# A hybrid decoder step on one core: the first norm taken on rows, and the FFN norm's root multiplied in behind the weights

## The chip, the cores and the metric

One core of a Trainium2 chip runs one launch of the kernel. The metric is the device time of a launch in microseconds. A few engines are named throughout: TensorE (PE; PEld is its weight load), VectorE (DVE), ScalarE (ACT), GpSimd (POOL) and SyncE (SP), whose queue issues most DMAs.

## The reference

The reference is one layer of a decoder for 512 prompt tokens and 8 sample tokens (T = 520), in float32, with D = 1024 and D_FF = 2816. What the change touches is this:

```python
def rmsnorm(x, g, eps=1e-6):
    return x * rsqrt(mean(x * x, axis=-1) + eps) * g

xn = rmsnorm(x, norm_mix);  z = xn @ W_in          # 4 branches, gates: o_A .. o_D
x  = x + (sum_i sigmoid(gate_i) * (o_i @ W_branch_i)) @ W_out
x  = x + CrossAttn(rmsnorm(x, norm_cross), memory)  # ends with @ w_co
g, u = split(rmsnorm(x, norm_ffn) @ w_ffn_in)
x  = x + (silu(causal_dwconv3(g)) * u) @ w_ffn_out
y  = rmsnorm(x, norm_final)
```

The last rows of g before the convolution are an output too (the state of the FFN convolution). For a sample token the convolution's history comes from an input state.

## The kernel before, in words

Activations lie transposed: a tile has 128 channels on the partitions and all 520 tokens on the free axis, and `xT` holds the residual as 8 such tiles (index k). Every matrix product is made in "pieces": 128 columns of a weight matrix against all tokens, with the sum over up to 8 k. Weights (`raw`) and activations are each split in a rounded high part and a low part (the difference), and each k takes three products: high by high, high by low, low by high (L919 to L921). A piece with 8 k is thus 2 halves of 260 tokens x 24 products. ScalarE rounds the weights (`split`, L1171 to L1177), GpSimd or, for some kinds, VectorE subtracts (L776, L1662), two pieces ahead. The accumulators `pb` are two tiles of two halves, so tile m can start when tile m - 2 has been read out. The other PSUM tensor `sd` (its quarters are `s0` to `s3`) serves everything else.

The order of all work is written out in one list, `timeline()` (L216 to L340), that each engine's program walks and from which it takes its own part: `piece`, `evac` (read a tile out), `evac2` (its second step), `side` (one of the small steps of the list `SIDE`, L165), `nsq`, `nroot` and `napply` (a norm's squares, root and application), `tap`, `k` and `v` (one tap of a long convolution, one page of a cache). After each half piece one side step is taken. Each engine is strictly in this order. Pieces 0 to 3 are "fq", 4 to 11 "cv" and "cg", 12 to 23 "gx"; 132 to 139 are "co" (w_co, 4 k each), 140 to 183 alternate two "fg" (gate) and two "fu" (up) tiles of the FFN, and 184 on are "fo".

The prologue: SP loads the constants' first 256 columns, four row tiles of x (512 KB each, `xrow`), x_sample, the other constants, and the parameter rows (L676 to L701), then the weights. TensorE transposes x and the parameters through `sd` (L831 to L846) and VectorE copies them to `xT` and `cols` (L1950 to L1961). Then norm 0 runs: ScalarE squares each k (L1249), TensorE sums over the partitions with a matrix of ones (L863 to L868), ScalarE takes Ln and Exp (L1256, L1257), and per k VectorE multiplies x, gain and root, ScalarE rounds to `xh`, VectorE subtracts to `xl` (L1642 to L1650). Piece 0 waits per k for `xl`. The residual is stored to a scratch in HBM (L1511), as its place holds other things in between.

Side steps "sm" 0 to 3 compute the decay and gate scalars from 16 columns of w_in: 48 products, transposes, a chain on VectorE and ScalarE. They start at piece 2. "fqr" sends the sample's queries to HBM behind piece 4; GpSimd reads them back, and with them the cache pages' products (L791) and sums on VectorE (L1686) can start.

Norms 2 to 4 (`ADDED`) square on ScalarE, add on VectorE (`n_add`, L1979) and let TensorE sum only once. For norm 3, the squares of tile k come behind the read-out of "co" tile k; the last square, the root and the nine apply steps stand before the first "fg" piece (L299 to L301). An "fg" tile is read out by ScalarE three times (tail, times the last tap, plain copy for the conv; L1215 to L1220), then VectorE's conv (L1638), tanh on ScalarE (L1188), a product (L1597), and the "fu" tile's product with it (L1640), rounded and subtracted to `hh` and `hl`.

## Time and profile before

| | |
|---|---|
| median of 3 runs | 1775.3 us (1775.08 to 1779.56) |
| the profiled execution's own time | 1775.84 us |
| its span, first to last instruction | 1773.0 us |
| mean granted TensorE clock | 0.91 of full |
| TensorE busy | 1512.1 us, 85% |
| VectorE busy | 918.6 us, 52% |
| ScalarE busy | 581.3 us, 33% |
| GpSimd busy | 557.2 us, 31% |

The stages follow each other, so a share over the whole span says little; what binds is read stage by stage. Times in the trace are microseconds from the span's start. TensorE's matmul rows show a duration with the pipeline's fill; what a product costs in a stream is the distance of two starts, or a stretch over its count.

### The profile page before, as it was taken

How to read it: one execution, taken by the hardware profiler on the slowest of the kernel's cores; microseconds unless marked ns; L12 is line 12 of the kernel's file. 1: busy time of each engine (PE TensorE's matmuls, PEld its weight loads, DVE VectorE, ACT ScalarE, POOL GpSimd, SP SyncE). 2: the span in 40 equal slices, each digit the busy share in tenths (PEclk: the TensorE clock that was granted, in tenths of full speed). 3: DMA queues.
4: the chain of work that ended last, by engine and by line, in shares of the span. 5: the costliest groups of instructions: out<-in, count | busy, mean ns of one | idle time of the engine just before them, and what ended most of it. 6: DMA issues, size and time to landing. Idle time of an engine off the chain costs nothing. (4 is left out here: it accounts for less than half of the span.)

```text
span 1773.0 us, 28178 instructions
## 1 busy us (share of the span) xinstructions
PE 1512.1 (85%) x11047; PEld 1396.2 (79%) x11047; DVE 918.6 (52%) x1286; ACT 581.3 (33%) x918; POOL 557.2 (31%) x310
## 2 busy tenths in 40 slices
PE   4886878688897988799888889888676999999995
PEld 3886877688897988776656659888566999999995
DVE  5159896889968675433233332264335555552112
ACT  3322560212133223433221232444324334433222
POOL 2255545343342333011111014310412444343440
PEclk9898996899998999899888879999877999999998
DMA  7144523433342444267544426433322333332331
GB/s 220 48 111 121 144 74 89 126 105 107 105 146 84 143 113 136 56 193 223 145 129 125 137 74 198 126 95 107 114 66 66 90 96 96 89 91 79 91 99 49
DMA packets 254643, 199.83 MB, mean 113 GB/s; under 512 B 15780, under 2 KB 212957, under 8 KB 254104
## 3 DMA queue, kind: packets, MB, share of 16 engines
q1 hardware_dynamic: 234149, 169.47, 33.1%
q10 hardware_dynamic: 19371, 23.86, 4.1%
q0 software_dynamic: 992, 4.72, 0.8%
q8 instruction: 87, 1.43, 0.3%
q14 instruction: 44, 0.36, 0.1%
HBM read 187.89 MB, written 10.81 MB: 112 GB/s over the span
## 5 line engine op out<-in xcount | busy, mean ns | idle before, releaser
L822 PE MATMUL pb<-xh,wh 128*128 128x260 f32 x2176 | 650.7, 299 | 51.7 <-DVE xl L1555 22.6
L822 PE MATMUL pb<-xl,wh 128*128 128x260 f32 x2176 | 634.2, 291 | 0.0
L822 PE MATMUL pb<-xh,rawl 128*128 128x260 f32 x2176 | 632.5, 291 | 0.0
L776 POOL TENSOR_TENSOR rawl<-raw,wh 128x1024 fp32r<-128x1024 f32 (+2 forms) x152 | 339.4, 2233 | 909.5 <-ACT wh L1169 908.7
L822 PEld LDWEIGHTS pb<-xh,wh 128*128 128x128 f32 x2176 | 431.4, 198 | 66.5 <-issue 44.3
L822 PEld LDWEIGHTS pb<-xl,wh 128*128 128x128 f32 x2176 | 431.8, 198 | 0.7
L822 PEld LDWEIGHTS pb<-xh,rawl 128*128 128x128 f32 x2176 | 430.4, 198 | 0.0
L1169 ACT ACTIVATE wh<-raw 128x1024 fp32r<-128x1024 f32 (+2 forms) x208 | 201.6, 969 | 545.0 <-PE pb L822 493.4
L822 PE MATMUL sd<-ar 128*128 128x128 f32 (+7 forms) x1488 | 262.7, 389 | 95.6 <-DVE ar L1555 62.3
L822 PEld LDWEIGHTS sd<-ar 128*128 128x128 f32 (+4 forms) x1488 | 178.9, 193 | 141.0 <-issue 75.8
L791 POOL TENSOR_TENSOR ar<-ar 128x512 f32<-128x512 f32 x128 | 189.0, 1476 | 248.9 <-DMA ar<-in_cache_fox_k 226.1
L1575 DVE SCALAR_TENSOR_TENSOR ar<-ar,cols 128x512 f32<-128x512 f32 x88 | 93.8, 1066 | 72.5 <-ACT ar L1169 71.8
L822 PE MATMUL pb<-oh,wh 128*128 128x260 f32 (+1 forms) x384 | 119.0, 310 | 9.2 <-ACT ar L1169 7.2
L1679 DVE SCALAR_TENSOR_TENSOR ar<-xT,cols,ar 128x512 f32<-128x512 f32 x120 | 125.7, 1085 | 1.2
L822 PE MATMUL pb<-ol,wh 128*128 128x260 f32 (+1 forms) x384 | 113.2, 295 | 0.0
L822 PE MATMUL pb<-oh,rawl 128*128 128x260 f32 (+1 forms) x384 | 113.0, 294 | 0.0
L1662 DVE TENSOR_TENSOR rawl<-raw,wh 128x1024 fp32r<-128x1024 f32 (+1 forms) x56 | 68.3, 1219 | 79.2 <-ACT wh L1169 79.1
L822 PE MATMUL pb<-hh,wh 128*128 128x260 f32 x352 | 101.5, 288 | 2.6 <-DVE hl L1555 2.6
L822 PE MATMUL pb<-hh,rawl 128*128 128x260 f32 x352 | 100.7, 286 | 0.0
L822 PE MATMUL pb<-hl,wh 128*128 128x260 f32 x352 | 100.6, 286 | 0.0
L826 PE MATMUL sd<-cst,ar 128*128 128x128 f32 (+7 forms) x359 | 65.0, 305 | 41.7 <-ACT ar L1476 18.5
L1686 DVE TENSOR_REDUCE ar<-ar 128x8 f32<-128x512 f32 x128 | 84.8, 678 | 26.9 <-POOL ar L791 26.0
(174 smaller groups left out, 1685.8 us busy)
## 6 DMA issues: line engine op xcount, KB each, us to landing
raw<-in_w_in SPq DMA_DIRECT2D x80, 512.0 KB, 4.2
ar<-in_cache_fox_k SPq DMA_DIRECT2D x128, 256.0 KB, 2.8
ar<-in_cache_fox_v SPq DMA_DIRECT2D x128, 256.0 KB, 3.0
raw<-in_w_ffn_in SPq DMA_DIRECT2D x44, 512.0 KB, 3.9
raw<-in_w_branch SPq DMA_DIRECT2D x32, 256.0 KB, 3.1
raw<-in_w_ffn_out SPq DMA_DIRECT2D x16, 512.0 KB, 3.9
ar<-in_cache_mem_k ACTq DMA_DIRECT2D x1, 4096.0 KB, 19.1
raw<-in_w_out SPq DMA_DIRECT2D x8, 512.0 KB, 3.9
```

The lines of the kernel that those rows point to most:

```text
L776: pool.tensor_tensor(rawl[:, p % RING, 0:kt, :], raw[:, p % RING, 0:kt, :], wh[:, p % (AHEAD + 1), 0:kt, :].bitcast(F32), SUB).then_inc(lo ...
L791: own(pool.tensor_tensor(kring[:, i % 4, :], kring[:, i % 4, :], qb[:, :], MUL), prod_done)
L822: return pe.matmul(o, l, r, start=start, stop=stop, skip_group_check=True)
L826: return pe.transpose(o, i, ident[0:n, 0:n])
L1169: own(act.activation(o, i, f, **kw), st)
L1575: (st if j == width - 2 else dve_c).by(dve.scalar_tensor_tensor(out=y[:, 0:SEQ], in0=x[:, 4 - width + j:4 - width + j + SEQ], scalar=wcol( ...
L1662: dve.tensor_tensor(rawl[:, p % RING, 0:kt, :], raw[:, p % RING, 0:kt, :], wh[:, p % (AHEAD + 1), 0:kt, :].bitcast(F32), SUB).then_inc(lo. ...
L1679: dve_c.by(dve.scalar_tensor_tensor(out=oC[:, c, 0:SEQ], in0=g[:, j - 1:j - 1 + SEQ], scalar=w[:, j - 1:j], in1=oC[:, c, 0:SEQ], op0=MUL, ...
L1686: page_free.by(dve.tensor_reduce(sc[:, i, :], kring[:, i % 4, :].rearrange("p (h d) -> p h d", h=FH), AX, ADD))
```

## The change

Two edits.

**First norm.** SP loads the vectors and two weight tiles before the other constants. ScalarE squares each row tile of x with a sum along the row, takes the root of the 5 columns of sums, and ScalarE and VectorE scale the rows into a new tensor `xnr`. TensorE transposes the scaled rows into `pb`; ScalarE reads them with the gain into `xh`, VectorE computes gain times the same minus `xh` into `xl`. TensorE's transposes of the parameters follow, and only then piece 0. The raw residual is transposed in new side steps "xr" 0 to 5 behind pieces 2 to 4, in the place of "sm", which goes behind "fqr". The store to the scratch is in "xr" 5.

**FFN norm.** Without its root, the norm's apply is a gain per channel. It is done tile by tile behind the read-out of "co" (`gain`), so the FFN's products run on x times gain. The squares' sum and the root are taken behind the first half of the first "fg" piece. Every "fg" tile is multiplied with the root (`lrsx`) as VectorE reads it from PSUM, and the product silu(g) once more with the root, for the sake of u. The tail and the scaled copy move from ScalarE to VectorE.

The diff, cut to its core:

```diff
-BY_ACT = {"fq", "fk", "fv", "cv", "cg", "gx", "ac", "gateA", "gateB", "gateC", "gateD", "gz", "kv", "cq", "fg"}
+BY_ACT = {"fq", "fk", "fv", "cv", "cg", "gx", "ac", "gateA", "gateB", "gateC", "gateD", "gz", "kv", "cq"}
...
-SIDE = ([("AFTER", "fq", 0)] + [("sm", n) for n in range(4)]
+SIDE = ([("AFTER", "fq", 0)] + [("xr", n) for n in range(6)]
         + [("AFTER", "fq")] + [("fqr", n) for n in range(2)] + [("KSTART",)]
+        + [("sm", n) for n in range(4)]
...
-    norm(0)
...
         if p == first_piece("fg"):
+            out.append(("gain", KD - 1))
             out.append(("nsq", 3, KD - 1))
-            norm(3, False)
...
             if kind == "co" and h == 1 and p > first_piece("co"):
+                out.append(("gain", p - first_piece("co") - 1))
                 out.append(("nsq", 3, p - first_piece("co") - 1))
+            if p == first_piece("fg") and h == 0:
+                out.append(("nsum", 3))
+                out.append(("nroot", 3))
...
+            own(pool.memset(zsam[:, :], 1.0), pool_made)
```

TensorE's prologue and the new side step:

```diff
+            pe.wait_ge(vec_in, 16 * 11)
+            pro_pe.by(tr(s3[:, 0:P], pv[:, B_VEC, :]))
+            pe.wait_ge(row_act.sem, 3)
+            for k in range(KD):
+                last = tr(s2[:, k * NB:(k + 1) * NB], xnr[0:NB, QT, k * P:(k + 1) * P])
+            pro_pe.by(last)
+            pe.wait_ge(row_dve.sem, 2)
+            for k in range(KD):
+                if k >= 4:
+                    pe.wait_ge(n_lo.sem, k - 3)
+                for t in range(QT):
+                    last = tr(pb[:, k % 4 // 2, k % 2, t * P:(t + 1) * P], xnr[:, t, k * P:(k + 1) * P])
                 pro_pe.by(last)
+            pe.wait_ge(par_in, 16 * 7)
+            for j in range(5):
+                if j == 2:
+                    pe.wait_ge(n_lo.sem, 1)
+                if j == 3:
+                    pe.wait_ge(pro_dve.sem, 1)
+                if j == 4:
+                    pe.wait_ge(n_lo.sem, KD)
+                for b in range(max(1, 4 * j), 4 * j + 4):
+                    last = tr((sd[:, j, :] if j < 4 else pb[:, 1, 1, :])[:, (b % 4) * P:(b % 4 + 1) * P], pv[:, b, :])
+                pro_pe.by(last)
...
+                if kind == "xr":
+                    for j in range(2):
+                        for t in range(QT):
+                            tr(sd[:, j, t * P:(t + 1) * P], xrow[:, t, (2 * n + j) * P:(2 * n + j + 1) * P])
+                        last = tr(s2[:, j * NB:(j + 1) * NB], xsrow[0:NB, (2 * n + j) * P:(2 * n + j + 1) * P])
```

ScalarE:

```diff
+            def gain(k):
+
+                if k == 0:
+                    act.wait_ge(kprod.sem, NB)
+                act.wait_ge(ev_all.sem, count(dve_tile, mt_of("co", k)))
+                n_hi.by(act.activation(xh[:, k, :], xT[:, k, :], ACT.Copy, scale=col(V_FFN + k)))
...
+            for t in range(QT):
+                act.wait_ge(x_in[t], 16)
+                act_c.by(act.activation(xnr[:, t, :], xrow[:, t, :], ACT.Square, accum_out=ssq[:, t:t + 1]))
+            act.wait_ge(x_in[QT], 16)
+            fn(xnr[0:NB, QT, :], xsrow[0:NB, :], ACT.Square, accum_out=ssq[0:NB, QT:QT + 1])
+            fn(rsq, ssq, ACT.Ln, scale=1.0 / D, bias=eps6[:, 0:1])
+            fn(rsq, rsq, ACT.Exp, row_rt, scale=-0.5)
+            row_act.by(act.activation(xnr[:, 0, :], xrow[:, 0, :], ACT.Copy, scale=rsq[:, 0:1]))
+            row_act.by(act.activation(xnr[0:NB, QT, :], xsrow[0:NB, :], ACT.Copy, scale=rsq[0:NB, QT:QT + 1]))
+            row_act.by(act.activation(xnr[:, 2, :], xrow[:, 2, :], ACT.Copy, scale=rsq[:, 2:3]))
+            split(0)
+            act.wait_ge(xs_gain.sem, 1)
+            fn(xh[:, :, SEQ:T], xsg, ACT.Copy, xs_gain)
+            for k in range(KD):
+                if k == 2:
+                    split(1)
+                act.wait_ge(pro_pe.sem, 3 + k)
+                n_hi.by(act.activation(xh[:, k, 0:SEQ], pb[:, k % 4 // 2, k % 2, :], ACT.Copy, scale=col(V_MIX + k)))
```

VectorE, the read-out of an "fg" tile, the new side step, the prologue and the gain:

```diff
                     elif kind == "fg":
-                        stt(pairA[:, s, :], pairB[:, s, :], 1.0, pairA[:, s, :], ADD, MUL, ev_all)
+                        stt(pairA[:, s, :], pairB[:, s, :], 1.0, pairA[:, s, :], ADD, MUL)
+                        tt(pairA[:, s, :], pairA[:, s, :], lrsx[:, :], MUL, ev_all)
...
                 elif kind == "fg":
+                    tt(both(cb[:, s, 3:3 + T]), x, both(lrsx[:, :]), MUL, mt_dve)
+                    cp(tail_ff[:, idx, :], cb[:, s, 3 + T - 10:3 + T])
+                    ts(pairA[:, s, :], cb[:, s, 3:3 + T], cols[:, B_FW, 2 * KF + idx:2 * KF + idx + 1])
                     conv(cb[:, s, :], pairA[:, s, :], FCW, lambda j: cols[:, B_FW, KF * j + idx:KF * j + idx + 1], fh[:, :, :, idx], ev_y)
...
+                if kind == "xr":
+                    for j in range(2):
+                        dve_c.by(dve.tensor_copy(xT[:, 2 * n - 2 + j, 0:SEQ], sd[:, j, :]))
...
+            for t in (1, 3):
+                row_dve.by(dve.tensor_scalar(xnr[:, t, :], xrow[:, t, :], rsq[:, t:t + 1], None, MUL))
...
+            for k in range(KD):
+                dve.wait_ge(n_hi.sem, k + 1)
+                n_lo.by(dve.scalar_tensor_tensor(out=xl[:, k, 0:SEQ], in0=pb[:, k % 4 // 2, k % 2, :], scalar=col(V_MIX + k),
+                                                 in1=xh[:, k, 0:SEQ].bitcast(F32), op0=MUL, op1=SUB))
...
+                elif e[0] == "gain":
+                    k = e[1]
+                    dve.wait_ge(n_hi.sem, 3 * KD + k + 1)
+                    stt(xl[:, k, :], xT[:, k, :], col(V_FFN + k), xh[:, k, :].bitcast(F32), MUL, SUB, n_lo)
```

## Rows read from the trace of the kernel before

**Rows 1.** Busy time by stage: stretch, its length, each engine's us (instructions), clock, DMA.

```profile
0.00:38.80 38.80, 17.23 (x92) 14.52 (x92) 17.91 (x31) 13.98 (x18) 8.89 (x14) 0.98 0.75 217
110.00:200.00 90.00, 69.72 (x514) 68.27 (x513) 86.74 (x89) 25.68 (x39) 54.60 (x30) 0.89 0.47 132
1318.00:1338.00 20.00, 20.00 (x168) 19.83 (x166) 11.40 (x19) 9.53 (x14) 10.45 (x7) 1.00 0.48 141
1380.00:1480.00 100.00, 100.00 (x840) 100.00 (x840) 51.86 (x51) 38.99 (x58) 41.86 (x18) 1.00 0.32 92
```

**Rows 2.** Timeline of the prologue: start, us, engine, line, operation, count, idle before.

```profile
10.79 7.08 PE L826 MATMUL sd<-cst,ar 8*128 8x8 f32 x40 [10.79 <-DMA ar<-in_x_sample]
32.37 1.28 ACT L1169 ACT_TABLE_LOAD   x1 [1.28 <-PE pb L822]
34.38 1.28 ACT L1169 ACT_TABLE_LOAD   x1
38.86 0.56 PE L822 MATMUL pb<-xh,wh 128*128 128x260 f32 x1 [6.57 <-DVE xl L1555]
48.75 0.57 PE L822 MATMUL pb<-xh,wh 128*128 128x260 f32 x1
49.99 0.42 PE L822 MATMUL pb<-xh,rawl 128*128 128x260 f32 x1
50.20 0.42 PE L822 MATMUL pb<-xh,wh 128*128 128x260 f32 x1
```

**Rows 3.** Line 826, PE, two stretches: duration ns min/median/max, first and last start.

```profile
L826 PE MATMUL sd<-cst,ar x20: 420/421/474, 11.7 to 15.8; 128*128 128x128 f32 x20
...
L826 PE MATMUL sd<-cst,ar x20: 272/273/300, 19.3 to 21.4; 128*128 128x128 f32 x20
```

**Rows 4.** Timeline between 78 and 109 us, TensorE, VectorE, ScalarE.

```profile
78.76 1.51 PE L822 MATMUL sd<-ar,cst 8*128 8x128 f32 x5 [3.46 <-DVE ar L1555]
...
106.03 0.69 DVE L1686 TENSOR_REDUCE ar<-ar 128x8 f32<-128x512 f32 x1 [21.88 <-POOL ar L791]
...
109.03 1.06 ACT L1169 ACTIVATE wh<-raw 128x1024 fp32r<-128x1024 f32 x1 [4.03 <-PE pb L822]
```

**Rows 5.** Timeline under w_co and up to the first FFN pieces.

```profile
1318.00 0.70 DVE L1561 SCALAR_TENSOR_TENSOR xT<-pb,xT 128x520 f32<-128x520 f32 x1 [3.38 <-PE pb L822]
...
1327.36 0.15 DVE L1564 COPY cols<-cols 128x1 f32<-128x1 f32 x1
1327.69 0.64 ACT L1249 ACTIVATE ar<-xT 128x520 f32<-128x520 f32 x1 [0.42 <-DVE cols L1564]
...
1333.53 2.42 POOL L776 TENSOR_TENSOR rawl<-raw,wh 128x1024 fp32r<-128x1024 f32 x1 [2.02 <-ACT wh L1169]
1334.23 2.27 DVE L1555 TENSOR_TENSOR ar<-ar 128x520 f32<-128x520 f32 x1 [0.96 <-ACT ar L1249]
...
1337.76 0.28 PE L822 MATMUL pb<-oh,rawl 128*128 128x260 f32 x1
1341.18 0.70 DVE L1555 TENSOR_TENSOR ar<-ar 128x520 f32<-128x520 f32 x1 [0.91 <-ACT ar L1249]
1341.94 2.10 PE L822 MATMUL sd<-ar,cst 128*128 128x260 f32 x4 [3.90 <-DVE ar L1555]
...
1366.13 1.06 ACT L1169 ACTIVATE wh<-raw 128x1024 fp32r<-128x1024 f32 x1 [5.41 <-PE pb L822]
```

**Rows 6.** DMA, first 40 us: GB/s in slices; one issue, its size.

```profile
GB/s 0 27 189 305 306 403 382 400 391 309 398 229 191 174 132 199 96 93 277 307 299 301 291 290 299 345 380 320 260 21 0 0 0 0 0 0 0 532 266 532
...
cst<-in_cst SPq DMA_DIRECT2D x1, 836.0 KB
```

**Rows 7.** VectorE: line 1671 (520 columns scaled), and two instructions of the timeline.

```profile
L1671 DVE TENSOR_SCALAR ar<-xT,cols x4: 549/549/1453, 115.6 to 341.5; 128x520 f32<-128x520 f32 x4
...
1350.50 0.76 DVE L1561 SCALAR_TENSOR_TENSOR ar<-xT,cols,ar 128x520 f32<-128x520 f32 x1
...
1414.40 1.63 DVE L1575 SCALAR_TENSOR_TENSOR ar<-ar,cols 128x512 f32<-128x512 f32 x1 [3.81 <-ACT ar L1169]
```

More of the change, by code:

```diff
@@ L198, in sums_before @@
 def sums_before(i):
-    return sum(1 if n in ADDED else KD for n in range(i))
+    return sum(1 if n in ADDED else KD for n in range(1, i))
 def adds_before(i):
@@ L583, in build @@
         pv = v(QKV, N_BLK, P)
[L584 removed]
+        xnr, xrow, xsrow = v(0, 5, D), v(G + 1600, QT, D), v(8800, D)
+        ssq, rsq, xsg = zsam[:, 0:5], zsam[:, 8:13], v(SQ, KD, NB)
         wsm = v(G, KD, 16)
@@ L722, in v_group @@
                     page("cache_fox_v", i, v_slot(i), v_in[i % 8])
-            for p in range(RING - 1):
+            for p in range(2, RING - 1):
                 weights(p)
@@ L936, in side @@
                     return
-                if sums[0] > 1 and kind != "ef":
+                if sums[0] and kind != "ef":
                     pe.wait_ge(n_rt.sem, sums[0])
@@ L1281, in side @@
                 kind, n = s[0], s[1]
-                works = act_works(s) or s in (("gs", 8), ("ml", 0)) or (kind == "x" and n > 0)
+                works = act_works(s) or s in (("gs", 8), ("ml", 0), ("xr", 5)) or (kind == "x" and n > 0)
                 if not works:
@@ L1290, in side @@
                 va, av = upto(to_act, K), upto(to_dve, K)
-                if kind == "sm" and n == 1:
+                if kind == "xr":
+                    store(xscr, xT[:, :, :].rearrange("p a b -> p (a b)"), xs_out)
+                elif kind == "sm" and n == 1:
                     fins = act.activation(both(zrow[0:16, :]), sd[0:16, 2:4, 0:TH], ACT.Copy)
```

153 lines of the change are left out of this document (68 added, 85 removed).

## The prediction

> **What bounds the kernel now.** I read the execution by stages first. TensorE is all but full in the FFN (100 us of work in 100 us), VectorE fills the stretch from 110 to 200 us, and TensorE does 17.2 us of work in the first 38.8 us [rows 1]. So an end-to-end gain is a start that comes earlier or a hole in TensorE that closes; anything added to VectorE is free only where it has room. The two edits lie at two such holes.
>
> The first hole is the prologue. The reader is to see in the timeline that TensorE begins at 10.79 us, when x_sample, the last of the rows of x, has landed, and that the first product with weights starts at 38.86 us. Its first half piece (24 products) takes until 48.75 us, because each k waits for one gain, one rounding and one subtraction, and only from there do the products follow closely [rows 2]. They do so at 0.21 us each at first (50.20 less 49.99) [rows 2], against 0.119 us each in the FFN (100 us over 840) [rows 1]: half the granted clock. The transposes show the same two levels, 420 and 272 ns [rows 3]. TensorE finishes piece 7 at about 109.0 us, where ScalarE's rounding of weights is released [rows 4].
>
> The second hole is the norm before the FFN. The last product of w_co starts at 1337.76 us, the sum over partitions at 1341.94 us, and the first FFN piece is done only at 1366.1 us, where the rounding that waits for it starts [rows 5]. A piece of 48 products needs 5.7 us.
>
> **The prologue, part by part.** *Removed:* eight squares, 32 float32 products of 260 columns, a root on 520 columns with two table loads of 1.28 us, and the k-by-k apply [rows 2]. *Added on rows:* five squares of 1024 columns with a sum, a root of 5 columns, five scalings shared by ScalarE and VectorE, 40 transposes into PSUM, and eight times a gain by ScalarE and a subtraction by VectorE that both read PSUM. *Moved:* 40 transposes of the raw rows with their copies go to side steps behind pieces 2 to 4; the four gate-weight steps go behind fqr.
>
> When does the dense work start? The loads of x are 2.1 MB behind 128 KB; the first nine slices of 1 us in the traffic row sum to some 2.7 MB, of which a part was the 836 KB of constants that now go last [rows 6]. I take x as landed at 9.0 us (bounds 8.5 and 10.8, the time of before). Then on ScalarE: two squares 2.1 us, two table loads and two short functions 3.0, three scalings 3.2 (each 1.06, the duration of 128x1024 in [rows 5]): 17.3 us. VectorE's two scalings (1.1 each, twice the 549 ns of 520 columns [rows 7]) end earlier. Eight small transposes and the sample's gain take 1.2 us: 18.5. The eight k are then paced by the slowest of three: TensorE 0.85 us at the lower clock for four transposes (7.08 us for 40 with their copies [rows 2]), ScalarE 0.65 plus one rounding of weights (1.06) between, VectorE 0.76 [rows 7]. That is 8 x 0.8 + 1.06 + 1.4 for the ends of the pipe = 8.9: the eighth low part at 27.4. Four parameter transposes that wait for it take 0.5 to 0.9: **first piece at 28.3 us**, dense at once, as all eight k are there. TensorE has then worked for about 9 us almost without a hole; in the kernel of before the same kind of start gave the fast transposes by 19.3 us [rows 3], so I take the higher clock, and add 1 us for what may be left of the lower.
>
> From there to the end of piece 7: 384 products x 0.119 = 45.7 us; the 40 raw transposes at the higher clock 4.4 us (0.11 each for 19 of [rows 3], twice that at the lower clock); and the gate-weight steps as they cost now. From 48.75 to 109.0 are 60.3 us, in which 24 products at the lower and 336 at the higher clock take 5.1 + 40.0; the other 15.2 are those steps with 48 products, a 3.46 us hole [rows 4] in which TensorE waits for the chain on VectorE and ScalarE, and the lower clock behind it. I take the hole unchanged, as the chain is the same and has one half piece of cover in both orders. Sum: 28.3 + 1 + 45.7 + 4.4 + 15.2 = 94.6 us against 109.0, **14.4 us earlier**. Bounds: 10 us (x at 10.8, chain slower by 2, low clock for 24 more products) and 18 us (no clock loss, shorter loads).
>
> Does this reach the end? VectorE's full stretch begins with the first page sum at 106.03 us [rows 4], fed by the query row that fqr writes, which is still behind piece 4, so it moves with TensorE. The 3.4 us of gate arithmetic that VectorE now does inside pieces 6 and 7 falls where it waited for that query, so I cost it at nothing; without this cover it costs 3.4 us. In the other direction TensorE reaches fqr still earlier than piece 8, which could hide the query's round trip: up to 3 us more, kept for the range. SP's queue now passes two weight loads ahead of the constants: needed at 26 us, loaded in the first 20 or so. The store of x for the scratch is needed only by the first memset, two pieces later. The added GpSimd memset of 16 columns is nothing.
>
> **The FFN norm, part by part.** *Removed:* nine apply steps between w_co and the FFN, and the wait for the root. *Added under w_co:* per tile one gain on ScalarE (0.64) and one subtraction on VectorE (0.76 [rows 7]). VectorE's chain per tile becomes 0.70 accumulate, 0.15 copy, 0.1, 0.64 gain, 0.1, 0.76 subtraction, 0.70 add and 0.1 between: 3.3 us [rows 5, 7]. TensorE gives a tile every 2.87 us (24 x 0.119). So VectorE falls behind, and it is late next.
>
> There is a second cost. At 1334.23 us a VectorE add of two SBUF operands took 2.27 us where the same takes 0.70, and it ended just behind a GpSimd subtraction that ran from 1333.53 for 2.42 us; the evacuations, which read PSUM, keep their 0.70 [rows 5]. So each of the two added SBUF instructions can be held up. The Trainium skill has this as a rule against the change (GPSIMD Engine Reference, section 2, Architecture, and SBUF — State Buffer, section "SBUF: two separate sides"): the two engines share a pair of SBUF ports under an exclusive lock, and a VectorE instruction with two SBUF inputs is fully blocked while GpSimd holds it. By that rule the trace agrees.
>
> I walked the eight tiles through with the GpSimd subtractions set 0.75 us behind each release of ScalarE: evacuations start at 1318.0 [rows 5], 1321.4, 1324.6, 1327.9, 1331.2, 1334.4, 1338.4 and 1342.1 (3.44 us apart; two of them held by the long weight subtractions). The last low part is there at 1344.6, TensorE has waited 3 us for it, the sum over partitions costs 1.0 (half of 2.10, which was at the lower clock [rows 5]) plus 0.7 wait, and 27 products 3.2: first piece done at 1349.5, with 0.8 for clock 1350.1 against 1366.1: **16 us earlier**. Bounds: 20.5 (no lag: w_co's end plus 5.7 and the sum), and 8 (every added instruction held, 4.2 us a tile, and the lower clock after it).
>
> *Added per gate tile of the FFN on VectorE:* a product from PSUM with the root (0.70), a tail copy, a scaling (0.55), a product of two SBUF tiles (0.70). Four pieces take 22.9 us; VectorE's two gate and two up tiles then need some 16 us with the ScalarE waits between, and its conv step is held to 1.63 us by GpSimd already now [rows 7]. A gate tile's PSUM is wanted back 5.7 us after its evacuation can start; the second of a pair is delayed by the first to about 3 us. So this costs nothing, by the cover of that 2.6 us; if it is gone, TensorE stops once per pair, 11 times. ScalarE gets three instructions fewer per tile. The root (two loads and 1.3 us, 4.0 in all) ends under piece 1.
>
> **Sum.** 14.4 + 16 = 30.4 us off the profiled execution of 1775.8 us: 1745.4. That execution is 0.5 us above the median of 1775.3, so the median goes to **1745 us** (1.7% faster).
>
> A second rule of the skill, on table loads (ScalarE: Activation LUTs, "What ACT_TABLE_LOAD costs"), puts a drain of about 1.38 us onto each 1.28 us load. With it the two loads of the row root would cost 2.8 us more and the sum be 27.6 us. The trace has the second load begin 2.01 us after the first, with the first's own 1.28 and a whole activation in between [rows 2]: no run here shows room for that drain, and the traced 1.28 stands. Either sum lies inside the forecast's own range below.
>
> **The rivals.**
> (a) *VectorE bound under w_co:* every added instruction is held, as the one of 2.27 us. For it: GpSimd works 10.45 of 20 us there [rows 1]. Against: in my walk VectorE often starts first. FFN gain 8: total 23 us, 1752.
> (b) *The early start is partly lost:* x lands no earlier, the clock is low into piece 0, and gate arithmetic queues behind the page sums on VectorE, which then holds TensorE's step: prologue gain 8, total 24, 1751. It covers also that a moved step simply meets the same wait later.
> (c) *The change doesn't do what it says in one half:* the norm of rows is as long as the old one, since rows need two passes over ScalarE. Total 16 to 18, 1758. Against: the sum over partitions and the slow apply (9.9 us for a half piece) do go.
> (d) *Slower:* the lock in each FFN cycle. Per four pieces GpSimd works 9.6 us (41.86 per 100 [rows 1]); if VectorE did nothing meanwhile and lost 0.5 us behind each hold, it would need 9.6 + 16 + 2.5 = 28 us for 22.9: 5.2 us x 11 = 57 us lost, 1802 in all. It decides for slower from 2.8 us per cycle (30.4 / 11). Against: half of VectorE's instructions read PSUM, and one that starts first should finish first. (That a held VectorE instruction waits for the whole of GpSimd's is what the skill's SBUF page says of the lock; taken at every instruction, it gives this case.)
> (e) A mild form of (d), 1 us per cycle: gain 20, 1755.
>
> **How the numbers follow.** Forecast (1738 to 1750) 0.6; (a) 0.12; (b) 0.1; (e) 0.06; (c) 0.05; (d) 0.03; still better than 1738 through the hidden query 0.04. Range 1737 to 1756: from both upper bounds nearly together with the query's 3 us (18 + 18 + 3) to (a) and (b) with a part of (e). Faster by over 0.3% (5.3 us, about what a measurement of this kernel can tell from no change) 0.94: all but (d) and the tails of (c) and (e), which give within 0.02 and, with (d), slower 0.04.
>
> **What would show it.** First product with weights near 28 us and close spacing at once; piece 7 done near 95 us; first FFN piece done some 16 us less late against w_co's start; evacuations of w_co 3.3 to 3.7 us apart; the FFN at 840 products per 100 us. Wrong if TensorE's share in the FFN falls below 98%, or if the stretch from piece 7 to w_co grows.

## The result and the profile after

The changed kernel takes **1734.25 us** (median of 4 runs, 1732.22 to 1735.71) beside 1775.19 for the kernel before (4 runs, 1773.79 to 1779.56): a ratio of 0.9765, 95% interval 0.9744 to 0.9785. The forecast was 1745 with a range from 1737 to 1756, so the change gained more than the range allowed. Repeated later (experiment h1), it took 1739.24 us (6 runs, 1730.57 to 1744.83), ratio 0.9806 [0.978, 0.9832]. All ten runs together have their median at 1735.4, the 15 runs of the kernel before that stood beside them at 1773.5: **38 us** gained, of 30.4 forecast. The profiled execution took 1732.22 us, its span is 1729.2.

Busy time by stage of the kernel after, answering to [rows 1]; the columns are the same, the second and third stretch lie 14 and 27 us earlier, as the work does:

```profile
0.00:38.80 38.80, 20.58 (x148) 19.75 (x149) 15.60 (x31) 23.17 (x34) 13.84 (x17) 1.00 0.78 210
96.00:186.00 90.00, 71.62 (x529) 70.31 (x527) 86.57 (x87) 27.51 (x40) 53.48 (x28) 0.89 0.45 128
1291.00:1311.00 20.00, 20.00 (x165) 19.89 (x164) 12.94 (x23) 12.59 (x19) 9.09 (x6) 0.98 0.45 131
1380.00:1480.00 100.00, 100.00 (x841) 100.00 (x840) 73.23 (x89) 30.59 (x36) 42.73 (x17) 1.00 0.31 91
```

The FFN is as full as before (841 products in 100 us), though VectorE now works 73.2 us of 100 in place of 51.9.

Timeline of the prologue of the kernel after, ScalarE and TensorE (start, us, engine, line, operation, count, idle before), with the end of piece 7 as its last row; it answers to [rows 2, 4]:

```profile
5.36 1.28 ACT L1529 ACT_TABLE_LOAD   x1 [5.36 <-DMA ar<-in_x_prompt]
6.65 1.06 ACT L1529 ACTIVATE ar<-ar 128x1024 f32<-128x1024 f32 x1
...
10.80 0.19 ACT L1529 ACTIVATION_READ_ACCUMULATOR ar<-ar 128x1 f32 x1
...
12.04 1.28 ACT L1195 ACT_TABLE_LOAD   x1
13.34 0.30 ACT L1195 ACTIVATE ar<-ar 128x5 f32<-128x5 f32 x1
13.66 1.28 ACT L1195 ACT_TABLE_LOAD   x1
...
28.32 0.37 PE L836 MATMUL pb<-xh,wh 128*128 128x260 f32 x1
28.52 0.28 PE L836 MATMUL pb<-xl,wh 128*128 128x260 f32 x1
28.64 0.28 PE L836 MATMUL pb<-xh,rawl 128*128 128x260 f32 x1
...
95.18 1.06 ACT L1195 ACTIVATE wh<-raw 128x1024 fp32r<-128x1024 f32 x1 [1.27 <-PE pb L836]
```

The first product with weights starts at 28.32 us, from the second on the products follow at 0.12 us, and piece 7 is done at 95.18 in place of 109.03: 13.9 us earlier.

Under w_co, VectorE, GpSimd, TensorE and ScalarE of the kernel after; it answers to [rows 5]:

```profile
1307.98 2.41 POOL L790 TENSOR_TENSOR rawl<-raw,wh 128x1024 fp32r<-128x1024 f32 x1 [2.29 <-ACT wh L1195]
1309.73 1.21 DVE L1605 SCALAR_TENSOR_TENSOR xl<-xT,cols,xh 128x520 fp32r<-128x520 f32 x1 [0.93 <-ACT xh L1284]
...
1315.25 0.70 DVE L1605 SCALAR_TENSOR_TENSOR xT<-pb,xT 128x520 f32<-128x520 f32 x1
1317.07 0.76 DVE L1605 SCALAR_TENSOR_TENSOR xl<-xT,cols,xh 128x520 fp32r<-128x520 f32 x1 [0.92 <-ACT xh L1284]
1317.88 0.39 PE L836 MATMUL pb<-xh,wh 128*128 128x260 f32 x1 [2.45 <-DVE xl L1605]
1318.62 1.69 PE L836 MATMUL sd<-ar,cst 128*128 128x260 f32 x4
...
1324.36 1.06 ACT L1195 ACTIVATE wh<-raw 128x1024 fp32r<-128x1024 f32 x1
```

The eight evacuations start between 1291.39 and 1315.25 us, 3.41 apart; TensorE waits 2.45 us for the last low part, and the rounding behind the first FFN piece starts at 1324.36.

To find the surplus I lined the two traces up by the starts of ScalarE's 208 roundings of weights (counted from 0 like the pieces; the nth is that of piece n's weights and stands two pieces ahead of it) and took the difference. It is 13.9 us at the 10th, 15.7 at the 96th, 20.3 at the 100th, 23.5 at the 131st, 25.6 at the 140th, 41.8 at the 143rd and 44.6 at the 207th. The two steps that were forecast are there (13.9, and 16.2 from the 140th to the 143rd). Nearly 12 us stand between the 10th and the 140th, where the diff seems to touch nothing. I call these 12 us the surplus.

### The profile page after: what moved, and what is told of

The parts are those of the page before. It is cut to its first block and busy times, and to the rows that moved or that the text cites. A ratio compares the mean times of both kernels' runs of the same rounds, so it can differ in the third digit from the quotient of the medians.

```text
span 1729.2 us, 28170 instructions
## 1 busy us (share of the span) xinstructions
PE 1486.3 (86%) x11055; PEld 1379.2 (80%) x11055; DVE 961.7 (56%) x1366; ACT 556.1 (32%) x858; POOL 563.1 (33%) x311
## 5 line engine op out<-in xcount | busy, mean ns | idle before, releaser
L836 PE MATMUL pb<-xh,wh 128*128 128x260 f32 x2176 | 642.0, 295 | 34.1 <-ACT ar L1195 16.6
L790 POOL TENSOR_TENSOR rawl<-raw,wh 128x1024 fp32r<-128x1024 f32 (+2 forms) x152 | 343.9, 2263 | 859.1 <-ACT wh L1195 858.5
L836 PEld LDWEIGHTS pb<-xh,wh 128*128 128x128 f32 x2176 | 425.1, 195 | 42.0 <-issue 28.7
L836 PEld LDWEIGHTS pb<-xl,wh 128*128 128x128 f32 x2176 | 425.3, 195 | 0.5
L836 PEld LDWEIGHTS pb<-xh,rawl 128*128 128x128 f32 x2176 | 424.7, 195 | 0.0
L836 PE MATMUL sd<-ar 128*128 128x128 f32 (+7 forms) x1488 | 258.8, 390 | 95.9 <-DVE ar L1599 63.3
L840 PE MATMUL sd<-cst,ar 128*128 128x128 f32 (+6 forms) x363 | 63.7, 291 | 48.9 <-ACT ar L1505 20.7
## 6 DMA issues: line engine op xcount, KB each, us to landing
ar<-in_cache_mem_k ACTq DMA_DIRECT2D x1, 4096.0 KB, 19.7
```

Source lines behind the costliest of these rows:

```text
L790: pool.tensor_tensor(rawl[:, p % RING, 0:kt, :], raw[:, p % RING, 0:kt, :], wh[:, p % (AHEAD + 1), 0:kt, :].bitcast(F32), SUB).then_inc(lo ...
L836: return pe.matmul(o, l, r, start=start, stop=stop, skip_group_check=True)
L840: return pe.transpose(o, i, ident[0:n, 0:n])
```

## The experiments

Time is the median, the ratio is to the kernel before with its 95% interval; a gain in us behind a ratio is worked out from the ratio, unless it says medians. The kernel before was run again beside each group of experiments, with medians from 1771.0 to 1776.1 us, so two times of different groups compare only within a few us. The letters of the theories are those of each run's expectation. For the first four runs, theory A tied the surplus to the early start, and theory B to something that does not depend on it (in e1 and e2, to the FFN edit).

**e1: the rows edit alone** (the FFN norm, its apply and the readers of the "fg" tiles as before).

```diff
-            out.append(("gain", KD - 1))
             out.append(("nsq", 3, KD - 1))
+            norm(3, False)
```

> Only the first norm on rows and the moved side steps; the FFN norm and the read-out of the gate tiles are as before. The two edits' own gains in the traces are 13.9 us (piece 7 done at 95.2 instead of 109.0 us) and 15.2 us (between w_co and the first FFN pieces), 29 of the 41 us. Theory A (TensorE's clock falls at other places once everything starts at another time, and that gives the other 12 us): up to the FFN this kernel starts each stage as the changed one does, so it is 14 us plus about 9 us faster than before: ratio 0.987. Theory B (the other 12 us belong to the FFN edit): 14 us, ratio 0.992.

Measured: 1752.72 us, ratio 0.9876 [0.9848, 0.9905], 22 us off (19.7 by medians): more than theory B's 14.

**e2: the FFN edit alone** (the prologue and the side steps as before).

```diff
-            norm(3, False)
+            out.append(("gain", KD - 1))
...
             if kind == "co" and h == 1 and p > first_piece("co"):
+                out.append(("gain", p - first_piece("co") - 1))
```

> Only the FFN edit on the kernel before: gains under w_co, root behind the first half piece, gate tiles multiplied with it. Theory A: the stages ahead of the FFN are untouched and start when they did, so the gain is the edit's own 15 us, or up to 18 with the clock drop at the FFN's end avoided: ratio 0.990 to 0.9915. Theory B: 15 + 12 = 27 us, ratio 0.985. If both edits' gains simply add up, this one and e1 give 41 us together.

Measured: 1758.87 us, ratio 0.9901 [0.987, 0.9932], 17.5 us off (13.6 by medians; its six runs span 1748.3 to 1762.5). In its trace the difference to the kernel before is -1.0 us at the 140th rounding and 14.9 at the 143rd: nothing in the middle. The surplus comes with the rows edit.

**e3: the changed kernel, started late.** Thirteen more squares of 1.06 us before the row root.

```diff
+            for _ in range(13):
+                fn(xnr[:, 0, :], xrow[:, 0, :], ACT.Square)
             fn(rsq, ssq, ACT.Ln, scale=1.0 / D, bias=eps6[:, 0:1])
```

> The changed kernel with 13 squares of a row tile (1.04 us each plus waits, about 14 us) more on ScalarE ahead of the row root, thrown away. Every stage from piece 8 to w_co then starts about when it started before the change. Theory A (the start time decides where the clock falls): the delay costs 14 us and gives the extra back: 22 to 26 us slower than the changed kernel, ratio to before about 0.990. Theory B (the extra belongs to the new order of steps, not to the start time): it costs just 14 us, ratio 0.984 to 0.985.

Measured: 1753.50 us, ratio 0.9884 [0.9858, 0.991], 19.3 us over the changed kernel's first 1734.25, but 14.3 over its repeat. By the times this decides nothing. Its trace does: piece 7 ends at 110.24 us, 1.2 later than before, and at the 100th rounding this kernel is still 7.7 us ahead. Theory A falls for most of the surplus.

**e4: the kernel before, once more.**

> The kernel before once more, for a second trace of it. If the places where TensorE's clock falls repeat from run to run, each stage's time and granted clock is within 1 us and 0.02 of the first trace (971.7 to 1056.2 at 0.78; the FFN's end 1600.9 to 1629.9 at 0.88). If they are chance, they differ by several us from stage to stage, and the total by up to the 6 us that its four runs span.

Measured: 1773.65 us, ratio 1.0002 [0.9983, 1.002]. Its trace and the first one of the same kernel drift up to 5 us apart and are within 1 us at the end. A single rounding's difference of less than that means nothing.

What e1, e3 and the changed kernel share against e2, e4 and the kernel before is the list of side steps. The planner emits an event of the cache's value pages ("v", a group of four; "vx", a row's end) at each side step but every seventh: `background("v", step_n[0] % 7 > 0)`. The change puts six new steps ("xr") in front. So the count is six higher at each later step, other steps are the seventh, and six page events (groups 0, 5, 10, 15 and 24 and the end of one row, in pieces 77 to 95) come half a piece earlier. The prediction did not follow this count.

**f1: the kernel before, with the page events of the changed one.**

```diff
-                background("v", step_n[0] % 7 > 0)
+                background("v", (step_n[0] + 6) % 7 > 0)
```

> The kernel before, with one number of the planner changed: the value pages of the cache are skipped at every seventh side step, and the count is moved on by six, as the six new side steps of the change do. So the six page events that the change moves by half a piece (four pages and the end of one row's query among them, in pieces 77 to 95) stand where they stand in the changed kernel; nothing else is changed. Theory P (the extra gain of the middle comes from this move): 9 us off, 1772.5 to about 1763.5, ratio 0.993 to 0.997, and the rounding of weights 100 comes about 8 us earlier than in the kernel before. Theory S (it comes from the earlier start, or from TensorE's clock falling elsewhere): within 2 us of the kernel before, ratio 0.999 to 1.001.

Measured: 1767.85 us, ratio 0.998 [0.9964, 0.9996], 3.5 us off (0.7 to 6.4): between theory P's 0.993 to 0.997 and theory S's 0.999 to 1.001, so the time alone settles little. The stretch where the traces part shows more. From the 98th rounding to the 100th TensorE does the last page steps, and behind piece 96 all that are left in one burst. Waits of TensorE's weight loads there, first the kernel before (engine, line, releaser: us in total, times, longest):

```profile
PEld sd L822 <- ACT ar L1359: 8.0, 3, 3.8
PEld sd L822 <- DMA ar<-in_cache_fox_v: 2.6, 2, 1.4
PEld sd L826 <- ACT ar L1359: 2.2, 1, 2.2
```

and f1:

```profile
PEld sd L822 <- ACT ar L1359: 7.7, 3, 3.8
PEld sd L826 <- ACT ar L1359: 2.4, 1, 2.4
```

TensorE's matmuls wait another 0.7 us for the same DMA before, and not at all in f1. It is the last group, 31. At event n SP loads group n + 1, once TensorE has used group n - 1 (L754 to L757 of the changed kernel), so group 31 is loaded when group 29 is used. Group 29's is a seventh event that moves, inside the burst, ahead of step "fox" 31 in place of behind it. TensorE's timeline before, where group 29's eight products are in the row of 12 at 1036.11:

```profile
1029.33 0.64 PE L822 MATMUL sd<-ar 128*128 128x128 f32 x2
1032.07 2.04 PE L822 MATMUL sd<-ar 64*128 64x512 f32 x2 [2.11 <-DVE ar L1555]
...
1036.11 2.89 PE L822 MATMUL sd<-ar 128*128 128x128 f32 x12
...
1046.90 1.02 PE L822 MATMUL sd<-ar 128*8 128x512 f32 x2 [0.24 <-DMA ar<-in_cache_fox_v]
```

and in f1, where they are in the row of 10 at 1027.27 (a row names the form of its first product only):

```profile
1027.27 1.36 PE L822 MATMUL sd<-ar 128*128 128x128 f32 x10
1029.76 1.09 PE L822 MATMUL sd<-ar 64*128 64x512 f32 x2 [1.13 <-DVE ar L1555]
...
1031.96 0.61 PE L822 MATMUL sd<-ar 128*128 128x128 f32 x4
```

Before, the last page of group 31 lands at 1046.85 us and TensorE takes it at 1046.90; in f1 it has landed at 1037.07. The six moves of half a piece bring nothing that shows: f1 leads the kernel before by 0.9 us at the 10th rounding, by 1.1 at the 98th and by 6.6 at the 100th.

The DMA waits are not the whole difference. The 185th of TensorE's 258 products in this stretch starts 45.1 us into it before and 42.6 in f1, and no DMA wait has come by then; group 29's products have filled a part of the wait for VectorE. So 2.5 of the 5.5 us come ahead of the DMA waits and 2.9 with them. The stretch as a whole, first before and then f1 (columns as in [rows 1]), has a lower granted clock before:

```profile
998.15:1056.23 58.08, 48.28 (x262) 30.27 (x255) 20.64 (x40) 12.01 (x23) 2.52 (x2) 0.79 0.40 122
997.07:1049.68 52.61, 43.20 (x262) 28.87 (x255) 20.63 (x40) 12.00 (x24) 2.53 (x2) 0.84 0.41 121
```

How much of either part is the wait itself and how much the clock, the runs do not separate.

**f2: the changed kernel, with the old page events** (`(step_n[0] + 1) % 7 > 0`).

> The changed kernel with the count of side steps put back by six where the value pages are skipped, so that each page event stands in the half piece where it stands in the kernel before. Theory P: the changed kernel's 1734.3 becomes about 1743 (8 to 10 us more; ratio to before 0.981 to 0.983), what the prediction had forecast for the whole change. Theory S: 1734.3 within 2 us, ratio 0.976 to 0.978.

Measured: 1738.34 us, ratio 0.9816 [0.9786, 0.9847]: 4.1 us over the changed kernel's first median, 0.9 under its repeat. The times alone leave it open. The stretch does not:

| 98th to 100th rounding | us |
|---|---|
| old page places: before, e4, e2, f2, h2 | 58.1, 59.3, 57.6, 57.8, 57.5 |
| new places: after, h1, e1, e3, f1 | 52.5, 52.7, 52.5, 52.7, 52.6 |

No kernel of one group comes near the other: **4.8 to 6.8 us**, some 5.5, with either prologue and either FFN, early or late. The edited variants below that keep the new places (f4, g1 to g3, h3, h4, i1, i2) have 52.5 to 52.7 there too. So theory P is shown for this stretch.

**f3: a page event at every side step** (`background("v", 1)`, on the changed kernel).

> The changed kernel with a value page at every side step and none skipped: the pages run up to four events further ahead, and fewer are left for the burst behind piece 96, where TensorE waits for VectorE's rounding of them. Theory P: the burst is shorter by the events that it no longer holds; some 5 us faster than the changed kernel, 1729 (ratio 0.972 to 0.976), or a loss if a page is asked for before it is loaded. Theory S gives no reason for a difference: 1734 within 2.

Measured: 1761.64 us, ratio 0.9927 [0.9898, 0.9955]: 26 us over the changed kernel's 1735.4. The 84th to the 92nd rounding now take 114 us in place of 104, and TensorE waits for the cache's DMA there too (4.7 us). Theory P had allowed for a loss if a page is asked for before it is loaded. So the place of the pages matters on both sides.

**f4: four more products behind each gate tile of the FFN**, with the changed kernel. My forecast had priced the FFN at nothing.

```diff
+                        for _ in range(4):
+                            tt(tmp, pairA[:, s, :], lrsx[:, :], MUL)
                         tt(pairA[:, s, :], pairA[:, s, :], lrsx[:, :], MUL, ev_all)
```

> The changed kernel with four more VectorE products of two operands in SBUF (128x520, 0.70 us each, into a scratch tile) behind each gate tile of the FFN, 5.6 us for every four pieces of 22.9 us. VectorE is busy 74.1 of 100 us there, 17.0 per four pieces, so it would be busy 22.6 of 22.9. Theory A (the FFN has this room and the lock on the shared ports costs nothing while it has): 0 to 10 us more in all, 1734 to 1744. Theory L (the lock already takes most of the room, so that VectorE loses more than its own time to GpSimd's 9.8 us of each cycle): at least 2.5 us per cycle over 11 cycles, 1762 or more.

Measured: 1825.32 us, ratio 1.0303 [1.0279, 1.0326]: 90 us over the changed kernel's 1735.4, 8.2 us for each of the 11 cycles of four pieces, in which VectorE got 5.6 us of work. That is theory L's side, and far beyond its 2.5 us.

**g1: VectorE pipelined under w_co.** Its subtraction and added square of tile k stand behind the evacuation of tile k + 1.

```diff
+            order, held = [], []
             for e in TIMELINE:
+                late = e[0] == "gain" and e[1] < KD - 1 or e[0] == "nsq" and e[1] == 3 and e[2] < KD - 1
+                (held if late else order).append(e)
+                if e[0] == "evac2" and MT_KIND[e[1]] == "co":
+                    k = PIECES[MT_LAST[e[1]]][4]
+                    order += [x for x in held if x[-1] < k]
+                    held = [x for x in held if x[-1] >= k]
+            for e in order:
```

> The changed kernel; under w_co VectorE alone takes the low part and the added square of tile k behind the evacuation of tile k+1, so that it never waits for ScalarE's gain of the tile it has just evacuated. Per tile that is 0.70 + 0.15 + 0.76 + 0.70 and some 0.15 between, 2.46 us, less than TensorE's 2.87. Theory A (VectorE's chain of 3.41 us per tile is what TensorE waits 2.45 + 0.80 us for at the first FFN piece): evacuations 2.87 us apart but where GpSimd holds one, and some 3 us less in all, 1731 (ratio to before 0.974 to 0.976). Rival L (the lock is what spaces them): they stay 3.3 or more apart and the time stays at 1734 within 1.

Measured: 1739.05 us, ratio 0.9835 [0.982, 0.9851]: no gain. Timeline of g1 under w_co, GpSimd, VectorE, TensorE:

```profile
1310.26 5.19 POOL L790 TENSOR_TENSOR rawl<-raw,wh 128x1024 fp32r<-128x1024 f32 x2 [2.21 <-ACT wh L1195]
1310.30 2.92 DVE L1605 SCALAR_TENSOR_TENSOR xl<-xT,cols,xh 128x520 fp32r<-128x520 f32 x1
1313.25 2.75 DVE L1599 TENSOR_TENSOR ar<-ar 128x520 f32<-128x520 f32 x1
1316.04 0.70 DVE L1605 SCALAR_TENSOR_TENSOR xT<-pb,xT 128x520 f32<-128x520 f32 x1
...
1317.00 0.36 PE L836 MATMUL pb<-xh,wh 128*128 128x260 f32 x1 [2.64 <-DVE xT L1605]
```

Neither theory was right as written. The evacuations before this are 2.5 to 3.4 us apart, so the chain did get shorter. But VectorE no longer waits for ScalarE while GpSimd works. It runs into both of GpSimd's long subtractions and loses 2.2 and 2.1 us, another 0.9 to 1.0 us behind each of three short ones, and TensorE waits 2.64 us as it waited 2.45.

**g2 and g3: one and two added products per gate tile**, in place of f4's four.

> The changed kernel with one more VectorE product of two operands in SBUF behind each gate tile of the FFN: 1.4 us for every four pieces, a quarter of what cost 91 us in all with four. Theory T (a threshold: VectorE is late by what its chain of the two gate tiles exceeds, and this is still under it): within 3 us of the changed kernel, 1732 to 1737. Theory L (each added microsecond is lost, with what GpSimd holds): 91 / 4 = 23 us, 1757.

> The same with two products behind each gate tile: 2.8 us for every four pieces, the point that the prediction names. Theory T: VectorE's room of 5.9 us of each 22.9 still covers 2.8, so at most 10 us, 1734 to 1744. Theory L: 91 / 2 = 45 us, 1780.

Measured: 1769.11 us (0.999 [0.9973, 1.0007]) and 1799.23 us (1.0163 [1.0146, 1.0179]): 34 and 64 us over 1735.4, so 3.1 and 5.8 us per cycle for 1.4 and 2.8 of added work. Theory T falls, and theory L's 23 and 45 us were too low. **One product of 0.70 us per gate tile leaves the kernel level with the one before.** How, a cycle in the timeline shows. VectorE and GpSimd in the changed kernel:

```profile
1434.29 2.39 POOL L790 TENSOR_TENSOR rawl<-raw,wh 128x1024 fp32r<-128x1024 f32 x1 [2.25 <-ACT wh L1195]
1434.98 2.25 DVE L1599 TENSOR_TENSOR hl<-ar,hh 128x520 fp32r<-128x520 f32 x1 [1.15 <-ACT hh L1195]
1440.01 2.54 POOL L790 TENSOR_TENSOR rawl<-raw,wh 128x1024 fp32r<-128x1024 f32 x1 [3.33 <-ACT wh L1195]
1440.33 2.76 DVE L1619 SCALAR_TENSOR_TENSOR ar<-ar,cols 128x512 f32<-128x512 f32 x1
1445.78 2.56 POOL L790 TENSOR_TENSOR rawl<-raw,wh 128x1024 fp32r<-128x1024 f32 x1 [3.23 <-ACT wh L1195]
1446.85 1.52 DVE L1608 COPY ar<-ar 128x10 f32<-128x10 f32 x1
```

and in g2:

```profile
1435.04 3.50 DVE L1599 TENSOR_TENSOR ar<-ar,lrsx 128x520 f32<-128x520 f32 x2
1435.44 2.54 POOL L790 TENSOR_TENSOR rawl<-raw,wh 128x1024 fp32r<-128x1024 f32 x1 [3.24 <-ACT wh L1195]
...
1443.09 3.50 DVE L1599 TENSOR_TENSOR ar<-ar,lrsx 128x520 f32<-128x520 f32 x2
1443.49 2.54 POOL L790 TENSOR_TENSOR rawl<-raw,wh 128x1024 fp32r<-128x1024 f32 x1 [5.50 <-ACT wh L1195]
```

In the changed kernel, four VectorE instructions per cycle end just behind GpSimd's: the conv step (2.76 for 0.75), `hl` (2.25 for 0.70 here, 1.26 for the other one) and the tail copy (1.52 for 0.17), together 5.5 us of hold. So the 17 us of each 22.9 that VectorE is busy are some 11.5 of work.

In g2, each gate tile's pair of products takes 3.50 for 1.44 us; with the conv step (2.76) and one `hl` (1.74) the holds make 7.2 us. Work and holds are then some 20 us of a cycle of 25.7 (the roundings stand 25.05 or 26.6 us apart, four by four), so VectorE still isn't full. What costs is where the hold falls. The second product of the pair starts 0.33 us behind GpSimd and is held for 2.07, the read-out of the first "fu" tile stands behind it, and TensorE waits for that read-out. VectorE and TensorE in g2:

```profile
1446.62 0.69 DVE L1599 TENSOR_TENSOR ar<-ar,pb 128x520 f32<-128x520 f32 x1
1447.46 0.36 PE L836 MATMUL pb<-xh,wh 128*128 128x260 f32 x1 [1.87 <-DVE ar L1599]
```

and busy time and clock right behind that wait, and later (columns as in [rows 1]):

```profile
1448.00:1451.00 3.00, 3.00 (x16) 3.00 (x15) 1.98 (x3) 1.75 (x3) 1.78 (x1) 0.50 0.25 74
1452.00:1455.00 3.00, 3.00 (x27) 3.00 (x27) 0.16 (x1) 0.00 (x0) 0.00 (x0) 1.00 0.00 0
```

There are two costs. From the 143rd rounding to the 184th, g2 takes 264.0 us and the changed kernel 234.8. Ten such stops of TensorE make 20.0 of the 29.2 us, and 8.4 are products at wider spacing, most of them while the granted clock is 0.50, which the changed kernel never shows in this stretch. In g3 the stops make 30.4 us and the slower products 19.5 of 50.4; in f4, 61.7 and 17.9 of 80.2.

**g4: the page events half a piece earlier still** (`(step_n[0] + 6) % 7`, on the changed kernel).

> The changed kernel with the count of side steps moved on by six once more: six other page events (pages 1, 6, 11, 20, 25 and one end of a row) come half a piece earlier, and the page loads that they release with them. Theory P (an event must come early enough for its page load to be there in the burst behind piece 96, where the placement of before waits 3.3 us for DMA, and not so early that the step asks for a page in flight, as with none skipped): between the two, 1730 to 1742; more than 1745 would say that this early side is already the costly one.

Measured: 1736.62 us, ratio 0.9805 [0.9788, 0.9823]. As good as the changed kernel, not better, as theory P allowed; the stretch takes 52.7 us.

**h1: the changed kernel, once more.**

> The changed kernel once more. Theory A (the 1734.3 of its first four runs is its median): 1734 within 2, ratio 0.976 to 0.979. Rival C (those four fell together at the fast end, as the variants that read 1737 to 1739 suggest): 1737 to 1740, ratio 0.980 to 0.983, so that 3 to 5 us of the surprise are the run's and not the change's.

Measured: 1739.24 us, ratio 0.9806 [0.978, 0.9832]. Rival C: a part of the surplus was in those four runs. The trace of h1 is 8.0 us slower than the first one with the same instructions. Of it, 4.2 us lie between the 10th and the 96th rounding and 4.1 between the 131st and the 140th, where TensorE waits for others between short groups of work. Busy time and granted clock from the 131st rounding to the 134th in h1 (columns as in [rows 1]):

```profile
1207.00:1295.90 88.90, 58.79 (x349) 47.68 (x348) 26.52 (x47) 29.19 (x73) 21.66 (x11) 0.77 0.27 95
```

and of the same stretch in the first trace of the changed kernel:

```profile
1202.20:1286.60 84.40, 53.97 (x350) 43.55 (x349) 26.49 (x47) 29.19 (x73) 21.66 (x11) 0.85 0.29 100
```

The same 350 products, 4.8 us more of TensorE's time at a clock of 0.77 in place of 0.85, and VectorE and ScalarE as before. The two levels of the clock fall differently over the same work from run to run.

**h2: the rows edit alone, with the old page events** (the edits of e1 and f2 together).

> The rows edit alone (the FFN as before), with each value page in the half piece where the kernel before has it. Theory P (the rows edit itself gives the 14 us of its prologue, the page move 4 to 8): 1757 to 1760, ratio 0.992 to 0.9935, against 0.9876 with the move. Rival (the earlier start itself brings more): 1752 to 1754, ratio 0.988 to 0.9895.

Measured: 1757.26 us, ratio 0.9909 [0.9885, 0.9933], the time that theory P gave: 15.5 us off by medians, against 19.7 with the pages moved (e1); by the ratios 16.1 against 22.

**h3 and h4: GpSimd idle in the FFN, with one and with four added products.** ScalarE writes a scaled copy where GpSimd subtracts, which leaves the low part of those weights out.

```diff
+                if p > first_piece("fg") + 1:
+                    act.wait_ge(lo.sem, p)
+                    act.activation(rawl[:, p % RING, 0:kt, :], raw[:, p % RING, 0:kt, :], ACT.Copy, scale=2.0 ** -13).then_inc(lo.sem, 1)
```

> The changed kernel with one added product behind each gate tile of the FFN, as in the run that cost 35 us, and with GpSimd idle from the third FFN piece on: in place of its subtraction ScalarE writes a scaled copy of the weights (1.06 us per piece), which leaves the low part of the weights out of the products. Theory L (the added microsecond costs because VectorE's two-operand instructions wait for GpSimd's): TensorE is full again, 840 products per 100 us, and the time is that of the changed kernel, 1732 to 1738. Theory T (VectorE's own chain is too long with it): stays above 1760.

> The same with the four added products (5.6 us per four pieces), which cost 91 us beside GpSimd. Theory L: VectorE's own time is then some 11.7 + 5.6 = 17.3 us of 22.9, so at most 10 us over the changed kernel, 1732 to 1745. Theory T: 1790 or more.

Measured: 1736.84 us (0.9806 [0.9782, 0.9831]) and 1739.24 us (0.9814 [0.9795, 0.9832]). That is theory L: what cost 34 us costs 1.4 over 1735.4, less than runs of one kernel differ, and what cost 90 us costs about 4. Busy time in the FFN of f4 (columns as in [rows 1]):

```profile
1400.00:1500.00 100.00, 80.47 (x621) 79.23 (x620) 79.41 (x94) 20.40 (x24) 32.00 (x13) 0.95 0.25 73
```

and of h4, with the same VectorE program:

```profile
1400.00:1500.00 100.00, 99.96 (x830) 99.52 (x829) 74.28 (x123) 46.47 (x51) 0.00 (x0) 1.00 0.31 91
```

VectorE does 123 instructions in 74.3 us beside an idle GpSimd, and 94 in 79.4 beside a working one.

**i1 and i2: VectorE takes the subtractions of the FFN's gate and up weights itself**, in the changed kernel and in g2.

```diff
-LOW_BY_DVE = ("gateA", "brA", "gateC", "brC", "fk", "fv", "gz", "kv", "cq")
+LOW_BY_DVE = ("gateA", "brA", "gateC", "brC", "fk", "fv", "gz", "kv", "cq", "fg", "fu")
```

> The changed kernel, in which VectorE subtracts the low part of the weights of the gate and up pieces in GpSimd's place (128x1024, 1.23 us each, four per 22.9 us). VectorE's own 11.7 us and 4.9 make 16.6 of 22.9 with nothing held. Theory L: TensorE stays full, 1736 within 4, neither better nor worse, as TensorE is the bound. Rival Q (the subtraction stands in VectorE's queue in front of a read-out that TensorE wants): 1 us or more per cycle, 1750 or more.

> The same with the one added product behind each gate tile, which costs 35 us where GpSimd does the subtraction. Theory L: VectorE's 16.6 + 1.4 = 18.0 us of 22.9 still hold, 1736 within 5. Rival Q: 1765 or more, as with GpSimd.

Measured: 1739.88 us (0.9788 [0.9756, 0.9819]) and 1750.38 us (0.9849 [0.9813, 0.9885]). The subtraction takes VectorE 1.23 us and not GpSimd's 2.5, and i1 is as fast as the changed kernel with nothing held. The added product then costs 10.5 us in place of 34. This is more than theory L allowed and less than rival Q's 1765: in i2, TensorE makes 821 products in the 100 us from 1400, against 834 in i1. What holds it there was not looked into. No version here beats the changed kernel.

## Why the prediction was right and wrong

**The prologue: right.** 14.4 us forecast for the end of piece 7, 13.9 measured (13.1 in h1's trace). By the medians of h2 the whole kernel gains 15.5. The first product came at 28.32 us for 28.3. That it met so closely is luck in part, as two terms were off in opposite directions: x was there earlier than the 9.0 us that I took (the first square could start at 6.65, behind a table load that I had not counted), and the five squares then run one behind another to 12.0 us, each with another 0.19 us to read its sum, where I had two squares behind the landing, to 11.1. The products of piece 0 ran at 0.12 us from the second on, so the 1 us set aside for the clock was not needed.

The second table load begins 1.62 us after the first, with a load of 1.28 and an activation of 0.30 in between. The drain of 1.38 us that the Trainium skill puts onto each load (ScalarE: Activation LUTs, "What ACT_TABLE_LOAD costs") has no room there either, so the measured 1.28 stands.

**The FFN norm under w_co: right.** Forecast were evacuations 3.44 us apart, 3 us of TensorE's wait and 16 us in all; measured 3.41, 2.45 and 0.80, and 16.2 (from the 140th rounding to the 143rd, which took 33.7 us before and 17.5 after; 15.8 in h1 and in e2). (The working has a slip of 0.2: 1349.5 and 0.8 are 1350.3.) Rival (a) did not come, but not because VectorE mostly started first, as the walk had it: on seven of the eight tiles GpSimd's subtraction started ahead of VectorE's low part, and it was done, or nearly, while VectorE waited 0.93 us for ScalarE's gain. Only two low parts were held, to 1.21 and 0.95 us for 0.76. g1, which takes that wait away, shows that the rival lay close.

**The FFN at nothing: right in its number, wrong in its reason.** I costed it by "the cover of that 2.6 us". g2 shows that an added 0.70 us per gate tile is already past it. The cover was not 2.6 us of free time per tile, but an order in which GpSimd's holds, 5.5 us of each cycle, fall where no read-out that TensorE wants stands behind them. That it held for this change was luck by the reasoning given. Rival (d) was priced at 28 us for 22.9 and judged at 0.03; g2 runs a cycle in 25.7 us, f4 in 30.9. Part of that is a term which (d) did not have: TensorE's lower clock behind each stop. Its stated point of 2.8 us per cycle held: g2, at 3.1, ends level with the kernel before. The Trainium skill's rule of the exclusive lock (SBUF — State Buffer, "SBUF: two separate sides") agrees with every held row and with h3 and h4, where the holds go with GpSimd's work.

**What failed is a missing term.** The sum carried the 14.4 us unchanged from piece 7 to w_co. "Only moved" steps were costed where they stood, but not for the count that the planner keeps of them. Six steps more shift the skipped one in seven. Six page events come half a piece earlier, which alone shows no gain, and in the burst behind piece 96 group 29's event comes ahead of a step that it stood behind. There TensorE fills a part of a wait with its products, and group 31 is loaded in time. That gives 4.8 to 6.8 us in every pair of traces; in whole times, 3.5 us (0.7 to 6.4) alone in f1, and 4.5 between the medians of h2 and e1. The prediction had this term at nothing. With it the sum is 13.5 + 16 + 5.5 = 35 us, or 1740, inside the range; the repeat gained 33.6 by medians (1772.79 to 1739.24).

**The rest** is in part the spread of runs. The first four runs of the changed kernel were on the low side of its ten (1730.6 to 1744.8). The range's lower end had no allowance for that, and it took 18 us for the FFN norm where the working's own bound was 20.5; with that and the 3 us of the query it would have reached 1734. Against the 38 us of all runs some 3 us stay open. The traces point at the rows edit: in f2 and h2, which have it with the old page places, the lead grows by 3.7 and 4.1 us between the 10th rounding and the 140th, and in e2 and e4, without it, by -0.4 and 1.1. Single traces drift by as much, and no run here tests it. Why TensorE's clock falls differently over the same work was not settled. Between f1's 3.5 us in its whole time and the 5.5 in its stretch the runs can't decide, as the interval holds both.

## What to carry to other kernels

A planner that counts steps is changed by a step inserted anywhere; compare the two orders event by event, also far from the edit, and price what moved. An engine can have idle time and no room: what counts is whether something that the bound engine waits for stands behind a hold. Test the room by adding one instruction before relying on it. When two engines contend for ports, taking the work off one of them, even at more own time for the other, bought room in the FFN here (i2 loses 10.5 us to what cost g2 34). The one reordering tried, under w_co, bought none.

## What was not expected of the hardware

- A copy of 128x10 in SBUF, 0.17 us alone, took 1.52 us and ended with GpSimd's subtraction: not only two-operand instructions are held. VectorE's product of a PSUM and an SBUF operand took 0.70 us in every stretch looked at.
- Who starts first decides, even by hundredths of a microsecond: in g1 GpSimd started at 1310.26 and VectorE at 1310.30, and VectorE took 2.92 us for 0.76. In g2, the product that started at 1443.09, ahead of GpSimd's 1443.49, took its 0.70, and the one behind it 2.77.
- A stop of TensorE costs more than itself: in g2, behind 1.87 us of waiting, the granted clock was 0.50 and TensorE made 16 products in 3 us, against 27 a little later.
- Ten runs of one kernel lie between 1730.6 and 1744.8 us, and two traces of it differ by 4.8 us of TensorE's time over the same products, at granted clocks of 0.85 and 0.77.
